# Recurrent rounds of a two-block kernel: all keys' norms in the first preparation, decays and running sums in a new order, the inverse's known quarters by ScalarE

## The reference, cut to what matters

```python
    w_log = -jax.nn.softplus(-(w0[d] + jnp.tanh(xw) @ w_up[d])) - 0.5
    decay = jnp.exp(-jnp.exp(w_log))
    a = jax.nn.sigmoid(a0[d] + xa @ a_up[d])
    kk = _heads(k * k_k)
    kk = kk * lax.rsqrt(jnp.sum(kk * kk, axis=-1, keepdims=True) + 1e-12)
    k_mod = k * (1.0 + (a - 1.0) * k_a)
...
    def step(S, inp):
        w_t, k_t, v_t, kk_t, a_t = inp[:5]
        sa = jnp.einsum('bhvk,bhk->bhv', S, kk_t)
        S = (S * w_t[:, :, None, :] - sa[..., None] * (kk_t * a_t)[:, :, None, :]
             + v_t[..., None] * k_t[:, :, None, :])
```

## Time and profile before

| | |
|---|---|
| median of 3 runs | 1602.47 us (1597.59 to 1603.24) |
| the profiled execution | 1600.96 us, of which the span is 1598.9 us |
| PE busy | 1533.3 us, 96% of the span |
| DVE, ACT, POOL busy | 797.0, 335.7, 273.4 us |
| mean granted clock of PE | 0.98 of full speed |
| tail with the first preparation | 112 to 252 us |
| rounds 0, 1, 2 | about 252 to 342, 342 to 438, 438 to 534 us |
| second block | from about 550 us to the end |

### The profile page before, as it was taken

How to read it: one execution, slowest core, us unless ns; L and a number is a source line. 1 busy time by engine, 2 the same in 40 slices (tenths; PEclk the granted TensorE clock), 3 DMA queues, 4 the chain that set the end, 5 groups by cost and what they waited for, 6 DMA issues and landing times.

```text
span 1598.9 us, 32139 instructions
## 1 busy us (share of the span) xinstructions
PE 1533.3 (96%) x14083; PEld 1349.5 (84%) x14083; DVE 797.0 (50%) x1492; ACT 335.7 (21%) x712; POOL 273.4 (17%) x145
## 2 busy tenths in 40 slices
PE   7999999799799899999999999999999999999998
PEld 2667768688698688998888999998999888899997
DVE  2342334655652426667431866522766753186643
ACT  1102133534432301034400121000104430012000
POOL 3404001000000035762200000004466320000000
PEclk9999999899899899999999999999999999999999
DMA  9221330000011534434234444553443323444551
GB/s 361 101 89 69 129 109 3 2 3 19 2 43 68 134 106 158 158 109 152 110 109 155 159 158 167 183 154 106 158 159 125 140 106 122 141 158 163 181 183 41
DMA packets 110907, 191.68 MB, mean 120 GB/s; under 512 B 20888, under 2 KB 27296, under 8 KB 110640
## 3 DMA queue, kind: packets, MB, share of 16 engines
q1 hardware_dynamic: 109776, 188.29, 34.4%
q0 software_dynamic: 960, 1.33, 0.3%
q10 hardware_dynamic: 32, 0.01, 0.0%
HBM read 188.57 MB, written 1.05 MB: 119 GB/s over the span
## 4 chain that ended last, share of the span: by engine, by line
PE 86%; issue 3%; PEld 3%; DVE 3%; DMA 2%; ACT 1%; POOLq 1%; DVEq 1%; ACTq 0%; SPq 0%; PEldq 0%
PE psum L1382 22%; PE psum L1241 15%; PE psum L1216 13%; PE psum L938 6%; PE psum L863 4%; PE psum L1492 3%; PE psum L1237 3%; PEld psum L1511 2%; PE psum L1427 2%; PE psum L1099 2%; PE psum L1511 2%; PE psum L1531 1%; PE psum L1306 1%; PE psum L1350 1%; DMA arena<-in_x 1%
## 5 line engine op out<-in xcount | busy, mean ns | idle before, releaser
L1382 PEld LDWEIGHTS psum<-arena 128*128 128x128 f32 x3136 | 350.5, 192 | 0.1
L1382 PE MATMUL psum<-arena 128*128 128x128 f32 x3136 | 350.5, 274 | 0.0
L1241 PE MATMUL psum<-arena 128*128 128x128 f32 x2240 | 263.8, 277 | 5.3 <-POOLq L846 5.3
L1241 PEld LDWEIGHTS psum<-arena 128*128 128x128 f32 x2240 | 256.9, 193 | 13.8 <-issue 13.6
L1952 ACT ACTIVATE arena<-psum 128x512 f32<-128x512 f32 (+6 forms) x238 | 115.9, 493 | 650.6 <-PE psum L1382 176.7
L1216 PE MATMUL psum<-arena 128*128 128x256 f32 x928 | 202.6, 379 | 0.0
L1216 PEld LDWEIGHTS psum<-arena 128*128 128x128 f32 x928 | 175.3, 189 | 25.6 <-issue 0.3
L817 POOL TENSOR_TENSOR arena<-arena 128x1024 f32<-128x1024 f32 x12 | 28.2, 2352 | 569.7 <-DMA arena<-in_w_in 517.8
L938 PEld LDWEIGHTS psum<-arena 64*64 64x64 f32 x3072 | 92.6, 134 | 7.6 <-issue 5.4
L938 PE MATMUL psum<-arena 64*64 64x64 f32 x3072 | 96.6, 219 | 2.2 <-issue 2.2
L1511 PE MATMUL psum<-arena 128*128 128x256 f32 x336 | 73.4, 379 | 0.8 <-issue 0.8
(11 more groups left out here) (391 smaller groups left out, 1920.8 us busy)
## 6 DMA issues: line engine op xcount, KB each, us to landing
arena<-in_w_in SPq DMA_DIRECT2D x33, 2048.0 KB, 7.7
arena<-in_w_up SPq DMA_DIRECT2D x16, 2048.0 KB, 8.7
arena<-in_w_down SPq DMA_DIRECT2D x16, 2048.0 KB, 8.0
arena<-in_w_out SPq DMA_DIRECT2D x6, 2048.0 KB, 8.2
arena<-in_w_branch SPq DMA_DIRECT2D x6, 2048.0 KB, 7.6
arena<-in_mod_w SPq DMA_DIRECT2D x5, 2048.0 KB, 14.2
arena<-in_w_in SPq DMA_DIRECT2D x3, 1024.0 KB, 6.5
arena<-in_w_in SPq DMA_DIRECT2D x12, 256.0 KB, 4.8
```

Source lines behind the costliest of these rows:

```text
L1241: mm = pe.matmul(b[:, n * P:(n + 1) * P], left[:, k, n * P:(n + 1) * P], right[:, k, :], start=k == 0, stop=k == half - 1)
L1382: mm = pe.matmul(b[:, n * P:(n + 1) * P], left[:, k, n * P:(n + 1) * P], right[:, k, :], start=first and n == 0 and k == 0, stop=last and ...
```

## The change

All three rounds' key norms are computed in the preparation of round 0: ACT squares three tiles, PE makes the two further products (banks `kk1` and `kk2`) between the last HGRN projection and the pooling projection of stream T, and ACT takes three logarithms and three exponentials; rounds 1 and 2 read the result from `hz`. Direction 0's decays go from step 6 to step 4; direction 1's running sum stays in step 3, its small columns go to step 6, the growing decays to step 7, the falling ones to step 8. DVE's products with the keys (`keyed`) go from steps 6 and 7 to steps 8 and 9. The known quarters of `xf` are copied by ACT behind the last level's copies. Two DMAs get one more wait each (`corners_placed`, `e_keys`).

```diff
-         + [[("pv0", "D", 1), ("pv1", "D", 1)], ...
+         + [[("kk1", "A", 1), ("kk2", "A", 1), ("pv0", "D", 1), ("pv1", "D", 1)], ...
...
+        def norm_of(j):
+            return (rn, hz[:, 0, :], hz[:, 3, :])[j]
...
-            pe.wait_ge(sem("e_squared"), j + 1)
-            pe.matmul(take_bank(ep, f"kk_{j}"), cst("blocks"), rn, start=True, stop=True).then_inc(ep.filled, 1)
+            if j == 0:
+                pe.wait_ge(sem("e_squared"), 1)
+                pe.matmul(take_bank(ep, "kk_0"), cst("blocks"), rn, start=True, stop=True).then_inc(ep.filled, 1)
...
                     if c == 0:
                         rw.wait_emptied(pe, f"x6{d}_{j}")
+                        pe.wait_ge(sem("corners_placed"), j + 1)
...
+                    for i in (1, 2):
+                        pe.matmul(take_bank(tl, f"kk{i}_0"), cst("blocks"), px[:, i - 1, :], start=True, stop=True).then_inc(tl.filled, 1)
                     w = use_chunk(pe, 10)
...
-            ep.wait_filled(act, f"kk_{j}")
-            emptied(ep, act.activation(rn, bank(ep, f"kk_{j}"), ACT.Ln, bias=eps(1e-12)))
-            act.drain()
-            yield
-            act.activation(rn, rn, ACT.Exp, scale=-0.5)
-            done("e_norm")
-            yield
-            for d in range(2):
+            def growing(d):
                 act.wait_ge(sem("e_cumulated"), 2 * j + d + 1)
                 for c in range(4):
                     q = slice(c * P, (c + 1) * P)
                     act.activation(sw[:, d, q], sw[:, d, q], ACT.Exp, scale=-DECAY, bias=dmid[:, d, c:c + 1])
-                    if c >= 2:
-                        act.activation(pl[:, d, (c - 2) * P:(c - 1) * P], cl[:, d, q], ACT.Exp, scale=-DECAY, bias=dmid[:, d, c:c + 1])
+
+            def falling(d):
+                for c in (2, 3):
+                    act.activation(pl[:, d, (c - 2) * P:(c - 1) * P], cl[:, d, c * P:(c + 1) * P], ACT.Exp, scale=-DECAY, bias=dmid[:, d, c:c + 1])
                 act.activation(ecol[:, j % 2, d], ecol[:, j % 2, d], ACT.Exp)
                 act.drain()
                 for c in range(4):
                     q = slice(c * P, (c + 1) * P)
                     act.activation(cl[:, d, q], cl[:, d, q], ACT.Exp, scale=DECAY, bias=nmid[:, d, c:c + 1])
                 done("e_decays")
...
+            growing(0)
+            falling(0)
+            yield
+            yield
+            yield
+            growing(1)
+            yield
+            falling(1)
...
                 yield
+                if l == 6:
+                    act.wait_ge(sem("corners_ready"), j + 1)
+                    for d in range(2):
+                        for r in HALVES:
+                            copy(xf[r, d, :, r], xh[r, d])
+                    done("corners_placed")
...
             yield
+            if j == 0:
+                dve.wait_ge(sem("e_norm"), 1)
+            dve.scalar_tensor_tensor(kn, k, rc[:, j, 0:1], norm_of(j), ALU.mult, ALU.mult)
+            fence()
+            yield
+            keyed(0)
             yield
             ep.wait_filled(dve, f"bonus_{j}")
             emptied(ep, dve.tensor_tensor(bon[:, j, :], bank(ep, f"bonus_{j}")[:, 0:T], us[:, 6 + j, T:2 * T], ALU.mult))
+            keyed(1)
...
-                    if l == 6:
-                        for r in HALVES:
-                            dve.tensor_copy(xf[r, d, :, r], xh[r, d])
```

More of the change, by code:

```diff
@@ L308, in plan_of @@
 def plan_of(pool):
-    return [(f"{g}_{j}", e, n) for x, j, k in order_of_streams() for g, e, n in GROUPS[x][k] if pool_of(x, j, k) == pool]
+    return [(f"{g}_{j}", e, n) for x, j, k in order_of_streams() for g, e, n in GROUPS[x][k]
+            if pool_of(x, j, k) == pool and not (g == "kk" and j)]
 def padded(plan, banks=NB):
@@ L1780, in prepare_scalar @@
                 ep.wait_filled(act, f"btok1_{j - 1}")
-            act.activation(rn, us[:, 3 + j, :], ACT.Square, scale=rc[:, j, 0:1])
-            done("e_squared")
+            if j == 0:
+                for i, dst in enumerate((rn, px[:, 0, :], px[:, 1, :])):
+                    act.activation(dst, us[:, 3 + i, :], ACT.Square, scale=rc[:, i, 0:1])
+                done("e_squared")
             def gates(x, dst, name):
@@ L1826, in prepare_scalar @@
                 done("e_decays")
-                yield
+            if j == 0:
+                ep.wait_filled(act, "kk_0")
+                emptied(ep, act.activation(rn, bank(ep, "kk_0"), ACT.Ln, bias=eps(1e-12)))
+                for i in (1, 2):
+                    tl.wait_filled(act, f"kk{i}_0")
+                    emptied(tl, act.activation(norm_of(i), bank(tl, f"kk{i}_0"), ACT.Ln, bias=eps(1e-12)))
+                act.drain()
+                for i in range(JT):
+                    act.activation(norm_of(i), norm_of(i), ACT.Exp, scale=-0.5)
+                done("e_norm")
+            growing(0)
[6 more added lines that the diff above has]
+            falling(1)
             yield
@@ L2252, in prepare_vector, with cumulated @@
         def prepare_vector(dve, j, done, emptied, bc, fence):
-            yield
-            yield
             k = us[:, 3 + j, :]
-            for d in range(2):
-                if d == 0:
-                    dve.wait_ge(sem("e_gates"), j + 1)
+            def cumulated(d):
                 w, c = sw[:, d, :], cl[:, d, :]
@@ L2279, in prepare_vector, with keyed @@
                 done("e_cumulated")
[L2280 to L2289, removed]
+            def keyed(d):
                 dve.tensor_tensor(la[:, d, :], kn, la[:, d, :], ALU.mult)
@@ L2295, in prepare_vector @@
                 done("e_keys")
-                yield
+            yield
+            yield
+            dve.wait_ge(sem("e_gates"), j + 1)
+            cumulated(0)
+            levelled(0)
+            yield
+            cumulated(1)
+            yield
+            yield
+            yield
+            levelled(1)
+            for d in range(2):
+                dve.scalar_tensor_tensor(bt[:, d, :], us[:, j, T:2 * T], rc[:, j, 3 + d:4 + d], km[:, d, T:2 * T], ALU.mult, ALU.mult)
+            done("e_bonus")
+            yield
+            if j == 0:
+                dve.wait_ge(sem("e_norm"), 1)
+            dve.scalar_tensor_tensor(kn, k, rc[:, j, 0:1], norm_of(j), ALU.mult, ALU.mult)
+            fence()
+            yield
+            keyed(0)
             yield
```

6 lines of the change are left out of this document (added), and 2 rows, old and new, of the table GROUPS.

## The result

The changed kernel takes 1605.07 us (median of 15 runs), the kernel before 1598.19 in the same comparison (15 runs); the ratio of the two is 1.0028, 95% interval 1.0015 to 1.0041: slower by 0.3%, inside the 0.5% band, and 0.1 us from the forecast. The ratio says 4.5 us, the two medians differ by 6.9: one run of the changed kernel was disturbed (5941 us), but leaving it out moves that median only to 1604.84, and the rest of the difference between the two measures I can't derive from the runs. The profiled execution has a span of 1601.4 us against 1598.9.

The account below looks back on a forecast made before the run. PE, busy for 96%, was taken to lose time at the first `u` of two ends, behind ACT's list. Terms 1.2 - 0.2 + 0.8 + 0 + 2.0 = 3.8 us on 1600.96 gave 1604.8, forecast 1605, range 1598 to 1612.

Parts of the forecast that it names:

- just pays: Second chunk at end 0: DVE's lead covers the 2.07 us of `keyed` placed ahead of the states.
- C: Both ends: the gaps vanish as decays and quarters run before level 6 is ready; about 1582 us, chance 0.06.
- D: ACT's lists at both ends: Ln and Exp share a table, each list 2.6 us shorter; 1599.6 us, chance 0.03.
- A: Rounds and prologue: gains hold, costs hide, `keyed` disappears behind PE, clock stays high in end 1; 1598.5 to 1600, chance 0.22.
- B: End 1: the new stall drops the clock through level 6, +8.9 us instead of 2.0; 1611.7 us, chance 0.13.
- the quarters' term: ACT's list before the first right side: four copies of quarters at 0.63 us add 2.5 us.
- Prologue: First preparation: two more norm products on PE, partly hidden behind a weight transfer; cost 1.2 us, between 0 and 2.1.
- End 0: End of round 0: norm's product leaves, ACT's list lengthens, `keyed` delays the third chunk; gain 0.2 us.
- End 1: End of round 1: norm's product frees nothing, `u` starts 2.25 us later, third chunk comes late; loss 0.8 us.
- its clock: End 1, behind the new 3.1 us stall: low granted clock costs 0 to 3.7 us, taken as 2.0.
- End 2: End of round 2: DVE loses four copies, ACT gains 2.5 us, both under output products; 0.
- the likeliest case: Whole kernel: the forecast's own mechanism holds; 1601 to 1609 us, chance 0.56.

Follow-up runs that it names:

- quarters back: Changed kernel with the known quarters of `xf` copied by DVE again instead of ACT; ratio to the kernel before 0.9998.
- Quarters only: Kernel before with one edit, ACT's four copies of the known quarters in place of DVE's; ratio to the kernel before 1.0038.
- two loads: Changed kernel with direction 0's decays one step later, behind stream Q's Ln, so two table loads precede the first right side; ratio to the kernel before 1.0007.
- norms only: Kernel before with only the norms moved to the first preparation, plus the one DMA wait this needs; ratio to the kernel before 0.9979.
- products behind the states: Changed kernel with steps 8 and 9 one place later, DVE's products with the keys behind the second and third chunks' states; ratio to the kernel before 1.0086.

## Why the prediction was right, and where only its sum was

The mechanism held in nearly every point. PE's first `u` is released by ACT's list; the list is 11.4 long where 11.25 was summed; the waits of 9.2 and 10.3 stand where 8 to 10 was named; three loads, four copies of 2.55 together; a wait of 3.13 at yvar, named in advance; DVE as releaser at L1019, 0.98 where 1.0 stood at the third chunk, though at the second, where the lead "just pays" was written, it is 0.40. HGRN's first scores come 1.26 ahead of before by the round's own start, just under the 1.3 to 1.9. Rivals C and D are out by the waits and the loads; A fails because `keyed` shows at the carried products, the clock fell in end 1 and the prologue cost 1.1; B failed because the level came back after about 3.4 us, before level 6 (after 6.8 in the kernel with the quarters back, so the distance to B is not large). Quarters only and quarters back show the quarters' term, 2.65 where 2.5 stood; the kernel with two loads shows the 1.28; norms only shows that the norms alone are a gain, as the terms had it.

The terms against the pair of profiles:

- Prologue, +1.2: measured 1.1. Of the 2.24 at score 0, 1.16 are there at 94 us already (L1501 starts at 94.61, before at 93.45), ahead of any changed instruction. Score 0 spreads from 252.8 to 255.5 over the kernels with this prologue (without the one that waits in it) and stands at 251.8 and 253.1 in the two without, so 1.1 is no finer than about 1. It fits with the kernel with the quarters back, which comes 1.0 behind before (252.82).
- End 0, -0.2: measured +0.64, inside the bounds.
- End 1, +0.8, and its clock, +2.0: measured 3.36 together for 2.8. The clock took 1.55 of it (5.32 for 3.77).
- End 2, 0: +0.78 between score 2 and output. It is there before level 5 of round 2, so it isn't the quarters, and the kernel with two loads, whose round 2 is the same, takes 101.24 there where before takes 101.23. So it belongs to this execution; what it is I did not trace.
- The second block, no term: -3.15 and -1.7. This step was missing. The forecast took the rest of the program as fixed, and it is not, by up to 5 us, since the number and length of its low stretches differ from execution to execution.

So 3.8 was summed for the rounds and 5.9 measured there (7.02 less the 1.16 ahead of them), and the second block gave 4.8 back in that execution. That the median came within 0.1 us is luck: the forecast added 3.8 us to an execution of 1600.96 us, which lies 2.8 above the median that the kernel before has in the comparison, and the medians differ by 6.9. The ratio, 1.0028, puts the cost at 4.5 us, near the 3.8, and on 1600.96 that is within the likeliest case's range of 1601 to 1609.

## What to carry to other kernels

When one engine's wait is the end of another engine's list, write the list out with its table loads and ask of each entry who needs it before the wait ends: here the decays could go behind, and that alone took the ratio from 0.9998 to 0.9944, where the whole change moved it by 0.0028. Put what moves where its engine stands still and nobody queues behind it: 2.1 us of DVE work ahead of a put on which PE waits made a wait of 1.52, close ahead of one of 0.61 that was there already, and the half clock behind the two cost more than the waits. Work that is added to an engine's list ahead of such a wait (the quarters) costs its full length, whatever the other engine saves.

## What the runs showed that was not expected

- Behind a wait of 1.52 us and one of 0.61 in dense work the granted clock fell to 0.50 for about 13 us. Nine kernels have the wait of 3.13 at `yvar`, with the same instructions of PE around it: in six the level fell for about 3.4 us, in two (quarters back; products behind the states) for about 6.8, and in one not at all.
- Behind the same wait of 3.47 us in the second block the low level lasted about 3.4 us in three profiles, 6.8 in six and 10.2 in five. With the other low stretches of the second block it makes a few us of difference between programs that are equal from there on, and between executions of one program.
